# Two-layer hybrid trunk on one core: x also supplied by features, the first two weight chunks taken step by step for both token tiles, x at the seams turned by the DMA

## What is computed

```python
for l in range(2):
    x = x + 0.5 * swiglu(rmsnorm(x, norm_ffn1[l]), w_ffn1_in[l], w_ffn1_out[l])   # 1024 -> 2*2816 -> 1024
    u = rmsnorm(x, norm_mix[l])
    q, k, v, g, p, c, gates = split(u @ w_in[l])
    y_ret  = (retention(q, k, v, positions) * silu(g)) @ w_ret_out[l]
    y_pool = pool_mixer(p, w_pool[l], pool_scale[l])
    y_conv = conv_module(c, ...) @ w_conv_out[l]          # depthwise, 31 taps, layer norm, silu
    x = x + (sig(g0) * y_ret + sig(g1) * y_pool + sig(g2) * y_conv) @ w_out[l]
    x = x + 0.5 * swiglu(rmsnorm(x, norm_ffn2[l]), w_ffn2_in[l], w_ffn2_out[l])
return rmsnorm(x, norm_final)
```

## Time and profile before

| What | Value |
| --- | --- |
| Median of 3 runs | 1152.99 us |
| Profiled execution, its own time | 1152.98 us |
| Its span | 1151.1 us |
| Outside the span | 1.88 us (1152.98 - 1151.1) |
| PE busy | 1140.0 us, 99% |
| DVE busy, ACT busy | 780.0 us (68%), 608.7 us (53%) |
| DMA | 234.70 MB, mean 204 GB/s |
| Granted TensorE clock | 0.999 over the span |

### The profile page before, as it was taken

One profiled execution on the slowest core, in us unless ns is written; L12 is line 12 of the kernel. 1 busy time (PEld: TensorE's weight loads), 2 busy tenths in 40 slices (PEclk: granted clock), 3 DMA queues, 4 the chain that ended last, 5 costly groups with the idle time before them and its releaser, 6 DMA issues.

```text
span 1151.1 us, 13215 instructions
## 1 busy us (share of the span) xinstructions
PE 1140.0 (99%) x5150; PEld 939.9 (82%) x5150; DVE 780.0 (68%) x953; ACT 608.7 (53%) x703; POOL 41.9 (4%) x67
## 2 busy tenths in 40 slices
PE   8999999999999999999999999999999999999997
PEld 6888888888878888888888888888888788888886
DVE  6656465699997766655465656367999976565543
ACT  7655445453655565555365554364637356555442
POOL 2000000000100010000010000020001001000000
PEclk9999999999999999999999999999999999999999
DMA  9966564563754566756576757455638645676640
GB/s 368 323 196 218 182 235 170 218 177 134 247 211 170 196 204 208 239 167 231 185 260 194 231 188 233 173 212 174 201 119 262 231 146 191 221 242 205 174 183 37
DMA packets 92942, 234.70 MB, mean 204 GB/s; under 512 B 62912, under 2 KB 63296, under 8 KB 68048
## 3 DMA queue, kind: packets, MB, share of 16 engines
q1 hardware_dynamic: 90384, 226.78, 58.6%
q0 software_dynamic: 1648, 6.06, 1.7%
q10 hardware_dynamic: 848, 1.02, 0.3%
HBM read 218.11 MB, written 1.05 MB: 190 GB/s over the span
## 4 chain that ended last, share of the span: by engine, by line
PE 86%; DVE 10%; ACT 2%; issue 1%; DMA 0%; POOLq 0%; ACTq 0%; DVEq 0%; POOL 0%
PE acc L352 28%; PE acc L354 28%; PE acc L353 28%; DVE y L1236 4%; DVE w_lo L1036 3%; PE tr L412 2%; ACT w_hi L675 1%; ACT pin L822 0%; DVE gates L1311 0%; DVE gates L1256 0%; DVE ua L1292 0%; DVE qk L1301 0%; DMA ident_gain<-in_ident 0%; PE tr L482 0%; DVE sideT_lo L1354 0%
## 5 line engine op out<-in xcount | busy, mean ns | idle before, releaser
L675 ACT CAST w_hi<-raw 128x2048 fp32r<-128x2048 f32 (+1 forms) x206 | 379.1, 1851 | 260.4 <-PE acc L354 255.9
L1036 DVE TENSOR_TENSOR w_lo<-raw,w_hi 128x2048 fp32r<-128x2048 f32 (+1 forms) x206 | 448.4, 2211 | 95.0 <-ACT w_hi L675 94.9
L352 PE MATMUL acc<-w_hi,xT_hi 128*128 128x512 f32 x1184 | 466.3, 394 | 1.0 <-DVE w_lo L1046 0.6
L354 PE MATMUL acc<-w_hi,xT_lo 128*128 128x512 f32 x1184 | 461.3, 390 | 0.0
L353 PE MATMUL acc<-w_lo,xT_hi 128*128 128x512 f32 x1184 | 460.9, 389 | 0.0
L352 PEld LDWEIGHTS acc<-w_hi,xT_hi 128*128 128x128 f32 x1184 | 222.4, 188 | 47.1 <-DVE gates L1311 1.5
L354 PEld LDWEIGHTS acc<-w_hi,xT_lo 128*128 128x128 f32 x1184 | 222.2, 188 | 47.0
L353 PEld LDWEIGHTS acc<-w_lo,xT_hi 128*128 128x128 f32 x1184 | 222.5, 188 | 44.4
L1099 DVE SCALAR_TENSOR_TENSOR h<-acc,rs,silu_gate 128x256 f32<-128x256 f32 x88 | 42.5, 483 | 175.2 <-ACT silu_gate L731 175.2
L352 PE MATMUL acc<-w_hi,hT_hi 128*128 128x512 f32 x352 | 137.5, 391 | 0.0
L354 PE MATMUL acc<-w_hi,hT_lo 128*128 128x512 f32 x352 | 137.0, 389 | 0.0
(11 more groups left out here) (122 smaller groups left out, 568.2 us busy)
## 6 DMA issues: line engine op xcount, KB each, us to landing
raw<-in_weights SPq DMA_DIRECT2D x194, 1024.0 KB, 4.8
raw<-in_weights SPq DMA_DIRECT2D x10, 512.0 KB, 3.6
bias<-in_gate_bias POOLq DMA_DIRECT2D x6, 512.0 KB, 7.8
raw<-in_weights SPq DMA_DIRECT2D x8, 256.0 KB, 4.8
scale_row<-in_pool_scale POOLq DMA_DIRECT2D x2, 512.0 KB, 8.7
x<-in_x SPq DMA_DIRECT2D x3, 256.0 KB, 8.0
band<-in_band POOLq DMA_DIRECT2D x1, 768.0 KB, 6.2
hT_planes<-h_planes SPq DMA_TRANSPOSE x44, 3.1
```

The costliest lines, as they stand in the source:

```text
L352: nc.tensor.matmul(o, a_hi, b_hi, start=first, stop=False)
L354: return nc.tensor.matmul(o, a_lo, b_hi, start=False, stop=last)
L675: nc.scalar.copy(w_hi[:, hf % HIGHS, 0:n], raw[:, hf % RAWS, 0:n]).then_inc(hi_split, 1)
L1036: nc.vector.tensor_tensor(w_lo[:, hf % RAWS, 0:n], raw[:, hf % RAWS, 0:n], w_hi[:, hf % HIGHS, 0:n].bitcast(F32), ALU.subtract).then_inc(l ...
```

## The change

1. **The start.** The host also gives x by features, with the gains of the first norm ahead of it (`x_first`). ACT's queue loads it in four transfers (1, 1, 2 and 4 pieces k, with the gains before the first). ACT and DVE split piece k of both tiles at once (`first_x_high`, `first_x_low`), and PE turns nothing. The four halves of the first two chunks arrive, and are cast and subtracted, in 16 quarters of 128x512. `first_blocks` takes the two chunks piece by piece: for each k two hi·hi products (tiles 0 and 1), two lo·hi, two hi·lo. x by tokens is loaded after all 16 quarters, and is used only for the squares and the additions.
2. **The seams.** PE turns nothing. A quarter of x (512 features of one tile) is separated by ACT (`split_x`), turned by a DMA transpose in SP's queue and put together by DVE (`x_join`), in the same three buffers as h. The last two chunks before a seam run as (chunk, tile) = (n-1, 0), (n, 0), (n-1, 1), (n, 1), and the first two behind it as (m, 0), (m+1, 0), (m, 1), (m+1, 1) (`two_blocks`).
3. **Inside the mixer.** Four taps of the convolution are done later by DVE (18 and 8 become 14 and 12); `retained` stands ahead of one `sub`; the convolution's output product waits for each half of its lo part apart; `ub` of tile 0 is taken before a cast.
4. **The end.** In the last chunk, tile 1's columns 512 to 1023 are closed one chunk earlier and added; the last chunk's share goes to a free PSUM bank in two parts of 256 columns, each added, squared and weighted by itself.

```diff
+            def first_blocks():
+                for g in (0, 1):
+                    b = IN_BANK[g]
+                    for t in range(T):
+                        wait_acc_free(0, g, t, 0, b)
+                    for k in range(KT):
+                        w_high, w_low = weights(2 * g + k // 4, k % 4 * NB, NB)
+                        pe.wait_ge(first_hi, KT * g + k + 1)
+                        for t in range(T):
+                            nc.tensor.matmul(acc[:, t, b, :], xT_hi[:, k, tokens(t)], w_high,
+                                             start=k == 0, stop=False)
+                        if g == 0:
+                            pe.wait_ge(first_x_lo, k + 1)
+                        for t in range(T):
+                            nc.tensor.matmul(acc[:, t, b, :], xT_lo[:, k, tokens(t)], w_high,
+                                             start=False, stop=False)
+                        pe.wait_ge(first_lo, KT * g + k + 1)
+                        for t in range(T):
+                            mm = nc.tensor.matmul(acc[:, t, b, :], xT_hi[:, k, tokens(t)], w_low,
+                                                  start=False, stop=k == KT - 1)
+                            if k == KT - 1:
+                                done(mm, (0, g, t, 0))
+                        if k == 3:
+                            mm.then_inc(front_used, 1)
+            def two_blocks(l, g, norm, mid={}):
+                in_block(l, g, 0, norm)
+                in_block(l, g + 1, 0)
+                in_block(l, g, 1, norm, mid)
+                in_block(l, g + 1, 1)
...
+                if l + f == 0:
+                    first_blocks()
+                else:
+                    two_blocks(l, g0, norm)
+                for b in range(2, FB):
...
+                def step(i, t):
+                    ks = OUT_CHUNKS[i]
+                    if t == 0:
+                        pe.wait_ge(hT_lo_ready, (2 * l + f) * FB + ks[-1] // 2 + 1)
+                    if i == final and t == 1 and not after:
+                        last_products(l, g0 + FB + i, ks)
+                    else:
+                        wide(l, g0 + FB + i, g0 + FB, t, hT, ks, i == 0, i == final)
...
+                if after:
+                    for t in range(T):
+                        step(final - 1, t)
+                        step(final, t)
+                else:
+                    for i in (final - 1, final):
+                        step(i, 0)
...
+            def last_products(l, g, ks):
+                m = len(ks) // 2
+                for i, k in enumerate(ks):
+                    hf = l * HALVES + 2 * g + i // m
+                    mm = product(acc[:, 1, out_bank(0), :], hT(k, 1), weights(hf, i % m * D, NB),
+                                 False, i == len(ks) - 1)
+                done(mm, (l, g, 1, 0))
+                for part in (0, 1):
+                    for i, k in enumerate(ks):
+                        hf = l * HALVES + 2 * g + i // m
+                        mm = product(ret[:, part, 0:256], hT(k, 1),
+                                     weights(hf, i % m * D + NB + part * 256, 256),
+                                     i == 0, i == len(ks) - 1)
+                    done(mm, (l, g, 1, 1 + part))
             def side(k, t):
                 return sideT_hi[:, k, tokens(t)], sideT_lo[:, k, tokens(t)]
...
+                pe.wait_ge(conv_lo_ready, l * 2 + 1)
+                wide(l, M_CONV, M_CONV, 0, side, range(4), True, True,
+                     {(0, 1): lambda: pe.wait_ge(conv_lo_ready, l * 2 + 2)})
...
+                wait_tr_taken(pe, ("m", l, 0, 1))
+                wide(l, M_OUT + 1, M_OUT, 0, xT, range(4, 8), False, True)
                 wait_tr_taken(pe, ("m", l, 1, 0))
                 wide(l, M_OUT, M_OUT, 1, xT, range(4), True, False)
-                wait_tr_taken(pe, ("m", l, 0, 1))
-                wide(l, M_OUT + 1, M_OUT, 0, xT, range(4, 8), False, True)
...
-            keep_busy(6)
-            pe.wait_ge(ident_landed, 16)
-            turn_x(0, 0, 0, 0)
-            keep_busy(2)
-            turn_x(0, 0, 0, 1)
-            keep_busy(6)
+            keep_busy(9)
...
+            def turn_x(l, norm, t, c):
+                at = piece(l, norm, t, c)
+                sp.wait_ge(x_split, at + 1)
+                sp.wait_ge(x_joined, at)
+                sp.dma_start_transpose(xT_planes[:].rearrange("p a (g n) -> p (a g) n", n=P),
+                                       x_planes.rearrange("p a k n -> p (a k n)")
+                                       ).then_inc(x_turned, 16)
...
+                for at, norm in ((0, 0), (MIX, 1), (FFN2, 3)):
+                    if (hf // HALVES, norm) in SEAM:
+                        for ahead, t, c in ((2, 0, 0), (2, 0, 1), (5, 1, 0), (6, 1, 1)):
+                            if hf % HALVES == 2 * at + ahead:
+                                turn_x(hf // HALVES, norm, t, c)
...
+            with_gains = P * (KT + S)
+            act.dma_start(x_first[:, 0:KT + S],
+                          x_first_in[0:with_gains].rearrange("(p n) -> p n", p=P)
+                          ).then_inc(x_first_landed[0], 16)
+            for i, (k, n) in enumerate(((1, 1), (2, 2), (4, 4))):
+                a = with_gains + (k - 1) * P * S
+                act.dma_start(x_first[:, KT + k * S:KT + (k + n) * S]
+                              .rearrange("p (k n) -> p k n", k=n),
+                              x_first_in[a:a + n * P * S].rearrange("(k p n) -> p k n", p=P, k=n)
+                              ).then_inc(x_first_landed[i + 1], 16)
...
+            def first_x_high(k):
+                act.wait_ge(x_first_landed[(0, 1, 2, 2, 3, 3, 3, 3)[k]], 16)
+                nc.scalar.activation(xT_hi[:, k, :], first_x(k), ACT.Copy, scale=x_first[:, k:k + 1]
+                                     ).then_inc(x_hi_ready, 1)
...
+            def split_x(l, norm, t, c):
+                wait_x(l, norm, t, c)
+                act.wait_ge(x_turned, 16 * piece(l, norm, t, c))
+                nc.scalar.copy(x_planes,
+                               x[:, t, columns(c)].bitcast(U16)
+                               .rearrange("p (k n a) -> p a k n", k=4, a=2)).then_inc(x_split, 1)
...
-            def begin(l, norm, g):
+            def seam(l, norm, hf):
+                split_x(l, norm, 0, 0)
+                square(l, norm, 0)
+                split_x(l, norm, 0, 1)
+                x_high(l, norm, 0, 0)
+                cast(hf + 1)
+                cast(hf + 2)
+                x_high(l, norm, 0, 1)
+                split_x(l, norm, 1, 0)
+                cast(hf + 3)
+                split_x(l, norm, 1, 1)
                 x_high(l, norm, 1, 0)
+                cast(hf + 4)
+                square(l, norm, 1)
                 x_high(l, norm, 1, 1)
...
+                if l + f == 0:
+                    for t in range(T):
+                        square(l, 0, t)
+                    silu(l, f, 0, 0)
+                    cast(ahead(0) + 1)
+                    silu(l, f, 0, 1)
+                    cast(ahead(1))
+                    split_h(l, f, 0, 0)
+                    split_h(l, f, 0, 1)
+                    silu(l, f, 1, 0)
+                    cast(ahead(1) + 1)
...
+            def x_join(l, norm, t, c):
+                dve.wait_ge(x_turned, 16 * (piece(l, norm, t, c) + 1))
+                dve.wait_ge(x_lo_ready, piece(l, norm, t, c))
+                nc.vector.tensor_copy(hT_whole[:].rearrange("p k n -> p (k n)").bitcast(U16)
+                                      .rearrange("p (m a) -> p a m", a=2), xT_planes[:]
+                                      ).then_inc(x_joined, 1)
...
                 add_next(l, norm, 0, 0)
                 add_next(l, norm, 0, 1)
+                x_join(l, norm, 0, 0)
                 x_low(l, norm, 0, 0)
+                x_join(l, norm, 0, 1)
+                sub(hf + 1)
                 add_next(l, norm, 1, 0)
                 x_low(l, norm, 0, 1)
+                add_next(l, norm, 1, 1)
+                sub(hf + 2)
+                x_join(l, norm, 1, 0)
+                sub(hf + 3)
+                x_low(l, norm, 1, 0)
+                x_join(l, norm, 1, 1)
+                sub(hf + 4)
+                x_low(l, norm, 1, 1)
...
+                if l + f == 0:
+                    hidden(l, f, 0, 0)
+                    hidden(l, f, 0, 1)
+                    sub(ahead(1) - 1)
+                    sub(ahead(1))
+                    hidden(l, f, 1, 0)
...
-                conv_taps(l, 18)
+                conv_taps(l, 14)
...
-                conv_taps(l, 8)
+                conv_taps(l, 12)
```

More of the change, by code:

```diff
@@ L770, in ffn @@
+                for b in range(2, FB):
+                    silu(l, f, b - 1, 1)
+                    cast(ahead(b))
+                    split_h(l, f, b - 1, 0)
+                    split_h(l, f, b - 1, 1)
+                    silu(l, f, b, 0)
+                    h_high(l, f, b - 2)
+                    cast(ahead(b) + 1)
```

(20 more changed lines are left out.)

362 lines of the change are left out of this document (175 added, 187 removed).

## The result

The changed kernel takes 1173.6 us (median of 4 runs, 1169.5 to 1174.8), the kernel before 1153.05 (4 runs): a ratio of 1.0171, 95% interval 1.0158 to 1.0184. It is 1.7% slower, where 1139.7 us was forecast. The profiled execution has a span of 1172.1 us, 34.3 above the forecast span of 1137.8. Note the spread: 5.2 us over four runs, against 0.4 of the kernel before.

What follows compares the result with a forecast made beforehand. PE was taken as the bound, busy 1140.0 of 1151.1 us. Terms 9.2 + 1.5 + 2.3 + 0.3 = 13.3 us off gave a span of 1137.8, with 1.88 beyond the span 1139.7 us; range 1137.0 to 1144.5.

Steps and rivals of the forecast that it cites:

- no product is added and only their order changes: At the seams: PE loses only the turns, 9.2 us of work; products stay 0.227 us apart.
- The seams' work: At the five seams: 20 groups of four PE turns go, 0.46 us each, 9.2 us off.
- The seams' waits: At the seams: the new order hides separations, transposes and joins; waits taken as 0, at worst 11.5 us per seam.
- The margin of 1.5 us for half 3: In a seam's new chunks: half 3's lo part is ready at 6.6 us after the seam's zero, needed at 8.15.
- rival 1: At the seams: the third quarter's transpose lands 2 us later, costing 1 us per seam, 1144.7 us in all; chance 0.15.
- Rival 3: At the seams: two successive slow turns for tile 1; slower kernel beyond 5.3 us a turn, 1197 at 9.7; chance 0.03.
- Its sign of being wrong: At the seams: the forecast is wrong if a turn takes over 5 us.
- The start: Kernel start: first product at 5.4 us, product 109, needing half 5, from 35.05 to 33.6; 1.5 us off.
- rival 2: Start and mixer: the changes there give nothing, so the time is 1143.5 us; chance 0.1.
- The mixer: Inside the mixer: waits of 0.78 and 0.35 us before two products go in both layers, 2.3 us off.
- The end: Last chunk: narrower addition and square save 0.2 us each, 256-column products cost 0.15; 0.3 us off.
- The output chunk: Mixer's output, tile 0: merged values needed 5.4 us sooner; cost nothing, up to 2.3 us per layer if cover fails.

Runs made afterwards that it cites:

- the ring back: Changed kernel with the ring of weights and all laid behind it 128 bytes per partition further on, at the old kernel's byte: 1155.1 us.
- the third turn moved alone: Changed kernel with each seam's third DMA transpose issued ahead of the load of half 5 instead of behind it: 1164.7 us.
- both turns early: Changed kernel with the weight ring at its old byte and each seam's third and fourth transposes ahead of the load of half 5: 1141.0 us.
- the reorder on DVE: Changed kernel with the weight ring at its old byte and, at seams, DVE's subtractions of halves 3 and 4 ahead of the joins: 1165.6 us.

## Why the prediction was wrong

**The assumption that failed most is no term of the sum.** It said that no product is added and only their order changes, and took 0.227 us for every one. The change to `ident_gain` stands in no step of it; it is 128 bytes taken from under everything allocated behind it. The effect is shown from both sides: undone in the changed kernel it gives 18.5 us back, done alone in the kernel before it costs 16.2, in either case more than the whole gain that was forecast. But it is not the whole sign: with the ring back alone the kernel is still slower (ratio 1.0019), with the third turn moved alone too (1.0098). With the ring back and the third turn moved it is within the noise (0.999); with the fourth moved as well it is faster (0.9895).

**The seams' work: right.** With all turns hidden, from the first product with xT in the mixer to the first with hT in the last FFN takes 883.54 us (189.88 to 1073.42), against 893.92 before: 10.4 less, where 18 groups of 0.46 and the mixer's 2.3 make 10.6 (0.6 us of one st wait stayed).

**The seams' waits: wrong, by one number.** The step that failed is "its transpose stands in SP's queue behind a 1 MB load that starts at -1.4 and ahead of the next, and lands at 3.5". The load stood there, issued at -1.2 from the first seam's zero; but 3.5 is the landing of a turn that waits for no load. Two more loads, issued at -5.9 and -5.3, were ahead of it, the last one landed at 5.9, and the turn at 7.0. The margin of 1.5 us for half 3 was counted well: a landing 3.5 us later gave a wait of 1.7 there, and 2.1 to 2.8 at the other seams. This is rival 1 with its mechanism and place, but 2.4 us per seam for the 1 us it was given; its counter-argument, that the slow turn of the earlier trace rows stood behind eight loads and a seam has one or two, is what the runs refuted. Rival 3 feared two slow turns in a row; only the third was slow (the fourth, issued at 200.1, 6.6 us after the last load ahead of it, took 2.7 us), so turns beyond its limit of 5.3 us did not cost what it priced. Its sign of being wrong, a turn of over 5 us at a seam, came true at all five. And the clock behind a wait was in no step: 4.5 us.

**The start: right in its chain, wrong in what follows.** PE started at 5.87 (5.4 forecast) and the product for half 5, at 33.6 by forecast, came here (answering to the earlier trace rows):

```profile
5.87 1.19 PE L425 MATMUL acc<-w_hi,xT_hi 128*128 128x512 f32 x2 [0.66 <-ACT w_hi L772]
...
33.55 0.50 PE L383 MATMUL acc<-w_hi,xT_hi 128*128 128x512 f32 x1 [0.28 <-DVE w_lo L1165]
```

The chain to it ran as counted: cast of half 4 from 22.9, 1/rms at 28.1, its first step stretched (1.18 us) until DVE's subtraction ended, cast of half 5 to 30.4, subtraction from 31.2. The steps ahead of it were less exact: the first 96 products were through at 30.3 and not at 29.3. PE started 0.5 us later, and in place of the waits for x (2.1 us counted) nine of the first products started 0.43 us apart, although the granted clock reads 1.00 there. The chain of half 5 covered both. In the run with both turns early, where they start 0.23 us apart, the waits for x cost 1.8 us, and product 109 came at 34.3, its chain beginning 0.8 us later. The sum also stopped at that product: in the changed kernel half 7 then cost another 0.7 us. By the first product with hT the start had gained 0.2 us in the run with both turns early (130.04 for 130.25), not 1.5. That is the start's half of rival 2. That the squares sat in the chain of half 5 is shown by the run that took them out.

**The mixer: right.** 2.3 forecast, 2.7 measured alone. **The end: right.** From the first product with hT in the last FFN (1084.95 before, 1073.42 with both turns early) to the end of the span: 66.2 us before, 65.9 with both turns early, 0.3 less. **The output chunk** cost nothing, as said.

So the forecast of 1139.7 describes the changed kernel with its tiles where they were and its turns ahead of the loads (1141.0); the 1.3 us between them are about what the start fell short. It did not describe the kernel that was given.

## What to carry to other kernels

When a diff resizes any tile, write down which tiles behind it move, and compare the distance between a product's two operands before and after; check it in the profile by the mean duration of one product per group, which no view of waits shows. When a transfer is moved into a queue, count the bytes issued ahead of it on that queue at that very moment, and issue small urgent ones before large patient ones. A wait that is removed should be followed to the next piece in line: here the third turn's became the fourth's, and half 5's became half 7's.

## What the runs showed of the hardware

- A product with a 128x512 moving operand starts every 227.0 to 227.1 ns when both operands' addresses in a partition differ by a multiple of 256 bytes, and every 232.4 (off by 128) or 233.4 ns (off by 192) at the other distances tried: 2.3 to 2.8%, on 3456 products 18 us. Products with hT, which moved together with the ring, stayed at 226.7 to 226.9; hT_hi begins 98304 bytes, 384 x 256, behind the ring's start in every kernel here. Why the distance counts was not tried, nor smaller offsets.
- A DMA transpose of 128x1024 two-byte elements at a seam landed mostly in 2.7 to 3.2 us (the slowest in 4.1) with no load issued on SyncE's queue in the 4.9 us ahead of it, and in 5.8 to 8.6 us behind loads of 1 MB of which the last was issued 0.9 to 2.6 us ahead; then it landed 1.0 to 1.2 us after that load.
- The granted clock fell to 0.50 for 3.4 us behind some of PE's waits of 2.1 to 3.2 us: three of five in the changed kernel, one of five with the ring back, four of five with the reorder on DVE, none of those under 2 us. It stayed at 1.00 behind others of 2.65 to 3.25 us, so the length alone does not decide. Products started 0.43 us apart there, and each stretch cost 1.4 to 1.7 us. Programs with such waits spread by 3 to 9 us from run to run, the four without a seam wait by 0.5 to 1.5 over 4 runs each.
